# A hybrid encoder block with 64 experts on one core: gathers and scatters of all 128 rows under a bound, gate and up weights split by matrix

## The chip, the cores and the metric

One core of a Trainium2 chip runs the whole layer. The metric is device time in microseconds for one execution, the lower the better. The other cores of the chip are idle.

## The reference

One layer of a streaming encoder, on x of (1, 512, 1024) in f32. First a mixing sub-layer (mLSTM heads, sparse attention, output projection), which the change doesn't touch. Then the channel sub-layer, a mixture of experts, cut to its core here:

```python
scores = jax.nn.sigmoid(hf @ w_router)                    # (512, 64)
# group-limited top 8 of 64 experts per token -> eidx, gw
def body(y, args):
    tok_b, g_b, e_b = args
    xb = hf[tok_b]
    u = jax.nn.silu(xb @ w_gate[e_b]) * (xb @ w_up[e_b])
    yb = (u @ w_down[e_b]) * g_b[:, None]
    return y.at[tok_b].add(yb), None
shared = (jax.nn.silu(hf @ ws_gate) * (hf @ ws_up)) @ ws_down
```

512 tokens times 8 experts are 4096 rows over 64 experts, 64 on average. Routing depends on the data. Run on its own inputs, the reference sends 37 to 100 tokens to an expert: experts 0 to 3 get 59, 51, 73 and 37, experts 26 to 31 get 45, 83, 83, 76, 78 and 43. Each expert has a gate and an up matrix of 1024 x 256 and a down matrix of 256 x 1024, 1 MiB each in f32.

## The kernel before, in words

Three stages come first: input projection (`stage_in`), attention (`stage_attention`), output projection and routing (`stage_route`). They take the first 400 us. In `stage_route`, L1217 and L1220 already load the weights of experts 0, 1 and 3 and some down matrices, and L1417 copies the number of tokens of each expert into `count_tab`.

`stage_experts` takes the rest. It handles one expert after the other, e = 0 to 63, eight per turn of a hardware loop (`turns`, L1678). All engines run their own queue of instructions; semaphores tie them together. For expert e:

- **DVE** builds a 0/1 matrix `pick` (L1881), PE multiplies it with token numbers and gates (`find`), and DVE reads out row numbers and gate weights (L1581 to L1584). The first count(e) of the 128 places hold tokens in order, the others get the number 512 + place, beyond the last token.
- **GpSimd (POOL)** gathers these rows of the normalised input from DRAM into `xg` (`gather_rows`, L1586), four experts ahead. Each row is 4 KB and goes to one partition. The number of rows moved comes from the count: `count_of` (L1756) loads it from `count_tab` into a register, `by_size` (L1745) goes down a tree of branches to one of eleven instructions, for 48, 56, ... 128 rows.
- **PE** transposes the rows (L2024). ACT and DVE split them into a high part rounded to fp32r and the low rest (`xhi`, `xlo`, L1810 and L1905), and do the same with the weights (`whi` at L1802, `wlo` at L1901). The product x times gate and up is the sum of three fp32r products: hi hi, lo hi, hi lo.
- **PE** makes gate and up together (`gate_up`, L2034): 24 matmuls of 512 columns (256 of gate, 256 of up) into one bank. The work is split along the contraction: half 0 is chunks 0 to 3 of both matrices, half 1 is chunks 4 to 7. Weight loads from DRAM (`load_half`, L1570), high parts (`high_half`), low parts (`low_half`) and matmuls all go by these halves. A half of a matrix is 4 KB in a row of DRAM per partition.
- **ACT** makes the silu (L1818), DVE the product `u` (L1910), PE transposes it (L2042) and multiplies it with the down matrix in plain f32 (L2089, `s_dn`). ACT and DVE scale the result by the gate weights into `yb`, two buffers (L1851, L1954).
- **GpSimd** adds `yb` to the sums in DRAM with an accumulating scatter (`add_rows`, L1592), as many rows as the size chosen. Rows of the padding go to 128 spare rows behind the 512. Scatter e starts only when scatter e-1 has landed (`s_sc`, L1770), and `yb` of expert e is written only when scatter e-2 has landed. The last two experts are added from SBUF by PE instead.

Transfers of weights all go through SP's queue: four buffers for gate and up, four for down. SP waits until the low part of a half is made, then loads the same half of the expert four ahead; for the down matrix it waits for `s_dn`. Each transfer is spread over the core's 16 DMA engines. GpSimd's indirect transfers use another queue on the same 16 engines. At the end of the stage a last norm and a store follow.

## Time and profile before

| | us |
|---|---|
| median of 3 runs | 1129.77 |
| lowest and highest | 1128.4, 1130.07 |
| the profiled execution, its time | 1132.51 |
| the profiled execution, its span | 1130.7 |
| PE busy | 1037.0 (92%) |
| DVE busy | 836.9 (74%) |
| ACT busy | 521.8 (46%) |
| POOL busy | 234.5 (21%) |

The span runs from the first to the last instruction of one execution; the rest of its time lies around it. Busy time counts instructions that compute or, for POOL, that write the descriptors of an indirect transfer. PE's matmuls are pipelined and their ends are modelled, so PE's busy share is no measure of its speed; the distance of the starts of matmuls is. A DMA share is the mean over the 16 DMA engines of the time in which they had a packet; it can be a little over 1 where packets overlap. "In the median to landing" is the time from the issue of a transfer to its semaphore.

### The profile page before, as it was taken

How to read it: one execution, taken by the hardware profiler on the slowest of the kernel's cores; microseconds unless marked ns; L12 is line 12 of the kernel's file. 1: busy time of each engine (PE TensorE's matmuls, PEld its weight loads, DVE VectorE, ACT ScalarE, POOL GpSimd, SP SyncE). 2: the span in 40 equal slices, each digit the busy share in tenths (PEclk: the TensorE clock that was granted, in tenths of full speed). 3: DMA queues.
4: the chain of work that ended last, by engine and by line, in shares of the span. 5: the costliest groups of instructions: out<-in, count | busy, mean ns of one | idle time of the engine just before them, and what ended most of it. 6: DMA issues, size and time to landing. Idle time of an engine off the chain costs nothing.

```text
span 1130.7 us, 16022 instructions
## 1 busy us (share of the span) xinstructions
PE 1037.0 (92%) x4777; PEld 733.0 (65%) x4778; DVE 836.9 (74%) x1480; ACT 521.8 (46%) x610; POOL 234.5 (21%) x145
## 2 busy tenths in 40 slices
PE   1899997978998989999998999999999999899995
PEld 1898887657446447766775666667766666566662
DVE  4887899886665457787876787778787776676865
ACT  3425463364111145555554554555555454545542
POOL 0000000100000034353321323423222222342210
PEclk9899998989996999999999999999999999999998
DMA  9775300600948078999999999999999999999944
GB/s 358 244 277 178 101 1 1 229 14 13 388 186 327 27 249 269 356 344 343 338 366 348 323 333 344 345 337 329 324 338 333 346 308 339 304 328 334 340 113 152
DMA packets 82999, 297.60 MB, mean 263 GB/s; under 512 B 10799, under 2 KB 23131, under 8 KB 73437
## 3 DMA queue, kind: packets, MB, share of 16 engines
q1 hardware_dynamic: 69188, 259.12, 63.6%
q0 software_dynamic: 12208, 34.62, 13.4%
q10 hardware_dynamic: 1514, 2.97, 0.7%
q14 instruction: 68, 0.56, 0.1%
q8 instruction: 21, 0.34, 0.1%
HBM read 274.71 MB, written 24.12 MB: 264 GB/s over the span
## 4 chain that ended last, share of the span: by engine, by line
DMA 37%; PE 13%; issue 7%; POOLq 3%; DVE 3%; SPq 2%; ACT 1%; POOL 0%; DVEq 0%; ACTq 0%
DMA y_rows<-yb,row_numbers 28%; PE ps L2034 6%; DMA side<-in_w_exp_up 5%; PE ps L2089 4%; DMA main<-in_w_exp_up 2%; POOLq L1757 2%; DMA xg<-h_rows,row_numbers 1%; SPq L1573 1%; PE ps L2024 1%; PE ps L2134 1%; POOLq L1751 1%; ACT w_gate_up_hi L1802 1%; DVE main L2008 0%; DVE w_gate_up_lo L1901 0%; DVE pick L1881 0%
## 5 line engine op out<-in xcount | busy, mean ns | idle before, releaser
L1901 DVE TENSOR_TENSOR w_gate_up_lo<-side,w_gate_up_hi 128x2048 fp32r<-128x2048 f32 x64 | 146.8, 2294 | 78.9 <-ACT w_gate_up_hi L1802 78.8
L1901 DVE TENSOR_TENSOR w_gate_up_lo<-main,w_gate_up_hi 128x2048 fp32r<-128x2048 f32 x64 | 146.7, 2292 | 71.9 <-ACT w_gate_up_hi L1802 71.8
L1594 POOL DMA_INDIRECT y_rows<-yb,row_numbers x62 | 116.2, 1874 | 375.3 <-issue 311.4
L1802 ACT ACTIVATE w_gate_up_hi<-side 128x2048 fp32r<-128x2048 f32 x64 | 122.1, 1910 | 95.5 <-DMA side<-in_w_exp_up 54.1
L1802 ACT ACTIVATE w_gate_up_hi<-main 128x2048 fp32r<-128x2048 f32 x64 | 122.2, 1910 | 91.5 <-PE ps L2034 45.8
L2034 PE MATMUL ps<-w_gate_up_hi,xT_hi 128*128 128x512 f32 x512 | 144.7, 404 | 11.8 <-DVE xT_lo L1905 8.7
L2034 PE MATMUL ps<-w_gate_up_hi,xT_lo 128*128 128x512 f32 x512 | 137.6, 390 | 0.0
L2034 PE MATMUL ps<-w_gate_up_lo,xT_hi 128*128 128x512 f32 x512 | 137.3, 390 | 0.0
L2034 PEld LDWEIGHTS ps<-w_gate_up_hi,xT_hi 128*128 128x128 f32 x512 | 91.4, 189 | 32.1 <-issue 14.2
L2034 PEld LDWEIGHTS ps<-w_gate_up_hi,xT_lo 128*128 128x128 f32 x512 | 96.2, 188 | 21.1
L2034 PEld LDWEIGHTS ps<-w_gate_up_lo,xT_hi 128*128 128x128 f32 x512 | 96.1, 188 | 21.0
L1588 POOL DMA_INDIRECT xg<-h_rows,row_numbers x48 | 81.4, 1695 | 86.6 <-issue 68.1
L1810 ACT ACTIVATE xT_hi<-ps 128x1024 fp32r<-128x1024 f32 x64 | 65.4, 1023 | 46.4 <-PE ps L2024 46.4
L1905 DVE TENSOR_TENSOR xT_lo<-ps,xT_hi 128x1024 fp32r<-128x1024 f32 x64 | 78.0, 1218 | 11.8 <-ACT xT_hi L1810 11.6
L1851 ACT ACTIVATE yb<-ps,found 128x512 f32<-128x512 f32 x64 | 43.9, 685 | 56.9 <-PE ps L2089 36.6
L2024 PE MATMUL ps<-consts,xg 128*128 128x128 f32 x384 | 55.6, 289 | 12.1 <-DMA xg<-h_rows,row_numbers 12.1
L1881 DVE TENSOR_SCALAR pick<-consts,place_in_expert 128x128 bf16<-128x128 f32 x256 | 63.1, 320 | 0.8 <-PEq L1113 0.8
L2089 PE MATMUL ps<-maskb,uT 128*128 128x512 f32 x128 | 60.7, 619 | 0.0
L2089 PE MATMUL ps<-rows,uT 128*128 128x512 f32 x128 | 57.7, 593 | 1.0 <-DVE uT L1914 1.0
L2089 PE MATMUL ps<-main,uT 128*128 128x512 f32 x128 | 57.6, 592 | 0.0
L2089 PE MATMUL ps<-side,uT 128*128 128x512 f32 x128 | 57.6, 593 | 0.0
L1451 PE MATMUL ps<-side,catT 128*128 128x512 f32 x128 | 55.5, 593 | 1.1 <-PEq L730 1.1
(309 smaller groups left out, 1554.9 us busy)
## 6 DMA issues: line engine op xcount, KB each, us to landing
side<-in_w_exp_gate SPq DMA_DIRECT2D x60, 512.0 KB, 9.6
side<-in_w_exp_up SPq DMA_DIRECT2D x60, 512.0 KB, 23.9
main<-in_w_exp_gate SPq DMA_DIRECT2D x60, 512.0 KB, 9.9
main<-in_w_exp_up SPq DMA_DIRECT2D x60, 512.0 KB, 24.6
side<-in_w_ada SPq DMA_DIRECT2D x20, 1024.0 KB, 7.7
main<-in_w_exp_down SPq DMA_DIRECT2D x16, 1024.0 KB, 23.1
maskb<-in_w_exp_down SPq DMA_DIRECT2D x16, 1024.0 KB, 20.4
side<-in_w_exp_down SPq DMA_DIRECT2D x16, 1024.0 KB, 23.6
```

The costliest lines, as they stand in the source:

```text
L1451: ins = nc.tensor.matmul(ps[:, 2 * i + half, :], catT[:, f, i * P:(i + 1) * P], wout[:, f, 512 * half:512 * (half + 1)], start=f == 0, sto ...
L1588: return pool.indirect_dma_start(out=xg[slot][0:rows, :], out_offset=None, in_=G.h2_rows, in_offset=bass.IndirectOffsetOnAxis(ap=sidx[0:ro ...
L1594: return pool.indirect_dma_start(out=G.y_sums, out_offset=bass.IndirectOffsetOnAxis(ap=sidx[0:rows, n:n + 1], axis=0), in_=yb[0:rows, slot ...
L1802: nc.scalar.activation(whi[:, half], wgu[n % RING][:, :, HALF * half:HALF * (half + 1), :] .rearrange("p m c f -> p c m f"), ACT.Copy).the ...
L1810: nc.scalar.activation(xhi[:, :, :], ps[:, 0:2, :].rearrange("p b (c t) -> p (b c) t", t=P)[:, :, 0:CAP], ACT.Copy).then_inc(s_xhi, 1)
L1851: nc.scalar.activation(yb[:, n % 2, 0:512], ps[0:CAP, 4, :], ACT.Copy, scale=found[:, n, 1:2]).then_inc(s_ya, 1)
L1881: ins = nc.vector.tensor_scalar(pick[:, slot, i, :], k[:, K_IOTA:K_IOTA + CAP], posm[:, bass.ds(NT * e + i, 1)], None, ALU.is_equal)
L1901: nc.vector.tensor_tensor(wlo[:, half], src, whi[:, half].bitcast(F32), ALU.subtract).then_inc(s_wlo, 1)
L1905: nc.vector.tensor_tensor(xlo[:, :, :], ps[:, 0:2, :].rearrange("p b (c t) -> p (b c) t", t=P)[:, :, 0:CAP], xhi[:, :, :].bitcast(F32), AL ...
L2024: ins = nc.tensor.transpose(ps[:, c // 4, (c % 4) * P:(c % 4) * P + CAP], xg[n % RING][:, c:D:KC], ident[0:CAP, 0:CAP])
L2034: ins = nc.tensor.matmul(ps[0:CAP, 2 + slot, :], xp[:, HALF * half + c, :], wp[:, half, c].rearrange("p m f -> p (m f)"), start=half == 0 ...
L2089: ins = nc.tensor.matmul(ps[0:CAP, 4 + half, :], uT[:, n % 2, f, :], wd[n % RING][:, f, 512 * half:512 * (half + 1)], start=f == 0, stop=f ...
```

## The change

Two changes at once.

Rows: every gather and every scatter moves all 128 rows, and a bound on the row number (511) has the hardware drop those beyond it. The first four gathers did that already. The count table, the count look-up and the tree of branches go; GpSimd's loop holds no branch.

Weights: the two parts of the work are no longer halves of the contraction, they are the two matrices. Part 0 is gate, part 1 is up. Each is one transfer of 1 MiB with 8 KB in a row per partition, one high part, one low part, and 24 matmuls of 256 columns into a bank of its own (gate in bank 2 or 3, up in bank 6 or 7).

```diff
-        def load_half(eng, e, slot, half, s_half):
-            at = slice(HALF * half, HALF * (half + 1))
-            for m, w in enumerate((w_gate, w_up)):
-                eng.dma_start(wgu[slot][:, m, at, :], w[e].rearrange("(p c) f -> p c f", c=KC)[:, at, :]).then_inc(s_half, 16)
+        def load_matrix(eng, e, slot, m, s_landed):
+            w = (w_gate, w_up)[m]
+            eng.dma_start(wgu[slot][:, m], w[e].rearrange("(p c) f -> p c f", c=KC)).then_inc(s_landed, 16)
...
-        def add_rows(pool, slot, n, rows=CAP):
+        def add_rows(pool, slot, n):
-            return pool.indirect_dma_start(out=G.y_sums, out_offset=bass.IndirectOffsetOnAxis(ap=sidx[0:rows, n:n + 1], axis=0),
-                                           in_=yb[0:rows, slot, :], in_offset=None, compute_op=ALU.add)
+            return pool.indirect_dma_start(out=G.y_sums, out_offset=bass.IndirectOffsetOnAxis(ap=sidx[:, n:n + 1], axis=0),
+                                           in_=yb[:, slot, :], in_offset=None, compute_op=ALU.add,
+                                           bounds_check=SEQ - 1, oob_is_err=False)
...
                         pool.wait_ge(s_xp, e + 1)
                         pool.sem_inc(s_passed, 1)
-                        count = count_of(e + AHEAD)
-                        by_size(count, SIZES, lambda rows: gather_rows(pool, n % RING, (n + AHEAD) % UNROLL, rows).then_inc(s_g[n % RING], 16))
+                        gather_rows(pool, n % RING, (n + AHEAD) % UNROLL).then_inc(s_g[n % RING], 16)
...
                         pool.wait_ge(s_sc, SC0 + 16 * e)
                         pool.sem_inc(s_passed, 1)
-                        count = count_of(e)
-                        by_size(count, SIZES, lambda rows: add_rows(pool, n % 2, n, rows).then_inc(s_sc, 16))
+                        add_rows(pool, n % 2, n).then_inc(s_sc, 16)
...
-                    nc.scalar.activation(whi[:, half], wgu[n % RING][:, :, HALF * half:HALF * (half + 1), :]
-                                         .rearrange("p m c f -> p c m f"), ACT.Copy).then_inc(s_whi, 1)
+                    nc.scalar.activation(whi[:, m], wgu[n % RING][:, m], ACT.Copy).then_inc(s_whi, 1)
...
-                    act.wait_ge(s_gu, 2 * e + 2)
+                    act.wait_ge(s_gu, 2 * e + 1)
...
                 def multiply(e, slot):
                     dve.wait_ge(s_sg, e + 1)
-                    nc.vector.tensor_tensor(u[:, :], sg[:, :], ps[0:CAP, 2 + slot, DE:2 * DE], ALU.mult).then_inc(s_u, 1)
+                    dve.wait_ge(s_gu, 2 * e + 2)
+                    nc.vector.tensor_tensor(u[:, :], sg[:, :], ps[0:CAP, 6 + slot, DE:2 * DE], ALU.mult).then_inc(s_u, 1)
...
                     pe.wait_ge(s_xlo, e + 1)
-                    for half in range(2):
-                        pe.wait_ge(s_wlo, 2 * e + (half + 1))
+                    for m in range(2):
+                        pe.wait_ge(s_wlo, 2 * e + (m + 1))
+                        if m == 1 and isinstance(e, int) and e == 0:
+                            pe.wait_ge(s_sdc, NT)
                         for j, (xp, wp) in enumerate(((xhi, whi), (xlo, whi), (xhi, wlo))):
-                            for c in range(HALF):
-                                ins = nc.tensor.matmul(ps[0:CAP, 2 + slot, :], xp[:, HALF * half + c, :],
-                                                       wp[:, half, c].rearrange("p m f -> p (m f)"),
-                                                       start=half == 0 and j == 0 and c == 0, stop=half == 1 and j == 2 and c == HALF - 1)
+                            for c in range(KC):
+                                ins = nc.tensor.matmul(ps[0:CAP, 2 + 4 * m + slot, DE * m:DE * (m + 1)], xp[:, c, :], wp[:, m, c, :],
+                                                       start=j == 0 and c == 0, stop=j == 2 and c == KC - 1)
                         ins.then_inc(s_gu, 1)
...
                 gate_up(0, 0)
-                pe.wait_ge(s_sdc, NT)
                 transpose_x(0, 1)
```

The low part, the SP loop, the loads of stage_route and the order of ACT's and DVE's instructions follow the same split: `high_half`, `low_half` and `load_half` became `high_part`, `low_part_of` and `load_matrix` in the same places, with one semaphore for a landed gate matrix and one for an up matrix.

## Rows read from the trace of the kernel before

**Rows 1.** The page, parts 1 and 2: PE's busy time, the 40 slices.

```profile
PE 1037.0 (92%) x4777; PEld 733.0 (65%) x4778; DVE 836.9 (74%) x1480; ACT 521.8 (46%) x610; POOL 234.5 (21%) x145
...
DMA  9775300600948078999999999999999999999944
```

**Rows 2.** POOL's two indirect transfers by line: min/median/max ns; the scatter's landing.

```profile
L1594 POOL DMA_INDIRECT y_rows<-yb,row_numbers x62: 1389/1588/3484, 439.0 to 1098.7; - x62
...
DMA to landing us min/median/max: 4.2/8.6/11.6
...
L1588 POOL DMA_INDIRECT xg<-h_rows,row_numbers x48: 956/1110/3117, 401.5 to 1060.8; - x48
```

**Rows 3.** Windows of the expert stage, first to last scatter, and 500:1000.

```profile
core 0: us, PE busy (x) PEld busy (x) DVE busy (x) ACT busy (x) POOL busy (x), PEclk, DMA share, GB/s
...
439.02:1098.68 659.66, 637.61 (x2805) 441.39 (x2805) 502.14 (x780) 350.06 (x305) 211.67 (x120) 0.99 0.99 328
...
500.00:1000.00 500.00, 482.77 (x2136) 334.89 (x2135) 381.74 (x599) 266.73 (x232) 154.39 (x92) 0.99 1.02 334
```

**Rows 4.** PE: chain and timeline at 434 us; timeline of the projection at 107 us.

```profile
433.67 5.49 PE ps L2034 x24
...
443.68 1.18 PE L2034 MATMUL ps<-w_gate_up_hi,xT_hi 128*128 128x512 f32 x4
...
107.09 1.13 PE L667 MATMUL ps<-w_lo,hT_hi 128*128 128x264 f32 x8
108.06 1.13 PE L667 MATMUL ps<-w_hi,hT_hi 128*128 128x264 f32 x8
```

**Rows 5.** DMA queues, window 500:1000: packets, MB, share of 16 engines.

```profile
q1 hardware_dynamic: 32421, 141.68, 79.4%
q0 software_dynamic: 8725, 25.17, 22.0%
```

**Rows 6.** Chain that ended last, window 560:610: start us, us, what.

```profile
579.27 8.64 DMA y_rows<-yb,row_numbers
...
588.01 0.29 POOLq L1757
...
589.16 0.56 issue
...
589.97 10.18 DMA y_rows<-yb,row_numbers
```

**Rows 7.** Timeline of POOL, 380:440: two of the first four gathers.

```profile
402.96 1.01 POOL L1588 DMA_INDIRECT xg<-h_rows,row_numbers  x1 [0.30 <-issue]
...
416.04 1.00 POOL L1588 DMA_INDIRECT rows<-h_rows,row_numbers  x1 [0.77 <-POOL rows L1739]
```

**Rows 8.** DMA queue q1 in windows 20:28 and then 345:357: packets, MB, share.

```profile
q1 hardware_dynamic: 847, 3.27, 102.6%
...
q1 hardware_dynamic: 695, 5.04, 102.0%
```

**Rows 9.** Windows of 0.2 us in expert 3's gather (columns as in rows 3).

```profile
418.10:418.30 0.20, 0.20 (x3) 0.16 (x2) 0.00 (x0) 0.20 (x1) 0.00 (x0) 1.00 0.53 123
418.30:418.50 0.20, 0.20 (x3) 0.16 (x2) 0.00 (x0) 0.20 (x1) 0.00 (x0) 1.00 0.33 82
418.50:418.70 0.20, 0.20 (x3) 0.16 (x2) 0.00 (x0) 0.20 (x1) 0.00 (x0) 1.00 0.50 205
```

**Rows 10.** Chain that ended last, window 715:775: scatters of experts 27 to 30.

```profile
727.93 10.88 DMA y_rows<-yb,row_numbers
...
740.68 9.57 DMA y_rows<-yb,row_numbers
...
752.04 8.48 DMA y_rows<-yb,row_numbers
...
762.54 8.17 DMA y_rows<-yb,row_numbers
```

**Rows 11.** Groups by line: ACT's high part of weights in the `side` buffers.

```profile
L1802 ACT ACTIVATE w_gate_up_hi<-side 128x2048 fp32r<-128x2048 f32 x64 | 122.1, 1910 | 95.5 <-DMA side<-in_w_exp_up 54.1
```

More of the change, by code:

```diff
@@ L48 @@
 STEPS = (SEQ - 1) // CAP
-MEAN = SEQ * 8 // E_N
-SIZES = [*range(MEAN - 16, CAP, 8), CAP]
 QK_W = 2 * HEADS * DH
@@ L1215, in load_gate_up @@
             def load_gate_up(e):
-                for m, name in enumerate(("w_exp_gate", "w_exp_up")):
-                    sp.dma_start(G.w_gate_up[e][:, m], A[name][0, e].rearrange("(p c) f -> p c f", c=KC)).then_inc(G.s_wgu[e], 16)
+                sp.dma_start(G.w_gate_up[e][:, 0], A["w_exp_gate"][0, e].rearrange("(p c) f -> p c f", c=KC)).then_inc(G.s_wg[e], 16)
+                sp.dma_start(G.w_gate_up[e][:, 1], A["w_exp_up"][0, e].rearrange("(p c) f -> p c f", c=KC)).then_inc(G.s_wu[e], 16)
             def load_down(e):
@@ L1530 @@
 AHEAD = 4
-HALF = KC // 2
 def stage_experts(nc, A, G):
@@ L1584, in pick_rows, with gather_rows @@
             return nc.vector.scalar_tensor_tensor(sidx[:, n:n + 1], f, -1.0, pad[:, 0:1], ALU.add, ALU.add)
-        def gather_rows(pool, slot, n, rows=CAP):
-            return pool.indirect_dma_start(out=xg[slot][0:rows, :], out_offset=None, in_=G.h2_rows,
-                                           in_offset=bass.IndirectOffsetOnAxis(ap=sidx[0:rows, n:n + 1], axis=0),
+        def gather_rows(pool, slot, n):
+            return pool.indirect_dma_start(out=xg[slot], out_offset=None, in_=G.h2_rows,
+                                           in_offset=bass.IndirectOffsetOnAxis(ap=sidx[:, n:n + 1], axis=0),
                                            bounds_check=SEQ - 1, oob_is_err=False)
-        def add_rows(pool, slot, n, rows=CAP):
-            return pool.indirect_dma_start(out=G.y_sums, out_offset=bass.IndirectOffsetOnAxis(ap=sidx[0:rows, n:n + 1], axis=0),
-                                           in_=yb[0:rows, slot, :], in_offset=None, compute_op=ALU.add)
+        def add_rows(pool, slot, n):
+            return pool.indirect_dma_start(out=G.y_sums, out_offset=bass.IndirectOffsetOnAxis(ap=sidx[:, n:n + 1], axis=0),
+                                           in_=yb[:, slot, :], in_offset=None, compute_op=ALU.add,
+                                           bounds_check=SEQ - 1, oob_is_err=False)
         with ExitStack() as inner:
@@ L1602, in isem @@
                 return inner.enter_context(nc.semaphore(name))
-            s_wgu, s_wd = G.s_wgu, G.s_wd
-            s_wgu2 = [isem(f"second_half_landed{n}") for n in range(RING)]
+            s_wg, s_wu, s_wd = G.s_wg, G.s_wu, G.s_wd
             dch = isem("dve_chain")
@@ L1687, in _ @@
             def _(sp):
-                for n in range(RING):
-                    sp.sem_inc(s_wgu2[n], 32)
                 def step(t, n, ahead):
@@ L1743, in _ @@
                 pool.wait_ge(s_yw, 16 * NT)
-                def by_size(count, sizes, move):
-                    if len(sizes) == 1:
-                        move(sizes[0])
-                        return
-                    half = len(sizes) // 2
-                    with pool.If(count > sizes[half - 1]):
-                        by_size(count, sizes[half:], move)
-                    with pool.Else():
-                        by_size(count, sizes[:half], move)
-                def count_of(e):
-                    return pool.value_load(G.count_tab[0:1, bass.ds(e, 1)], min_val=0, max_val=SEQ)
                 def step(t, n, ahead):
@@ L1895, in read_found, with low_part_of @@
                     pick_rows(q, n, 6 + n % 2).then_inc(s_idx, 1)
-                def low_half(t, n, half):
-                    dve.wait_ge(s_whi, 2 * (UNROLL * t + n) + (half + 1))
-                    src = wgu[n % RING][:, :, HALF * half:HALF * (half + 1), :].rearrange("p m c f -> p c m f")
-                    nc.vector.tensor_tensor(wlo[:, half], src, whi[:, half].bitcast(F32), ALU.subtract).then_inc(s_wlo, 1)
+                def low_part_of(t, n, m):
+                    dve.wait_ge(s_whi, 2 * (UNROLL * t + n) + (m + 1))
+                    nc.vector.tensor_tensor(wlo[:, m], wgu[n % RING][:, m], whi[:, m].bitcast(F32), ALU.subtract).then_inc(s_wlo, 1)
                 def x_low(e):
@@ L2156, in build @@
         G.xt = sb("xt", [P, NT, D])
-        G.s_wgu = [ctx.enter_context(nc.semaphore(f"gate_up_landed{n}")) for n in range(RING)]
+        G.s_wg = [ctx.enter_context(nc.semaphore(f"gate_landed{n}")) for n in range(RING)]
+        G.s_wu = [ctx.enter_context(nc.semaphore(f"up_landed{n}")) for n in range(RING)]
         G.s_wd = [ctx.enter_context(nc.semaphore(f"down_landed{n}")) for n in range(RING)]
```

44 lines of the change are left out of this document (21 added, 23 removed).

## The prediction

> **What bounds the kernel now.** First the page's parts 1 and 2 [rows 1]: TensorE is busy 92% of the span and the DMA line stands at 9 through the expert stage. Two resources look full, so I read that stage alone. The 62 scatter-adds start between 439.0 and 1098.7 us [rows 2]; the window between them [rows 3] is 659.66 us for 61 experts, 10.81 us each, with PE busy 637.61 us and the 16 DMA engines at a share of 0.99. Is 10.81 PE's own pace? No: when it waits for nothing, one expert takes PE 443.68 - 433.67 = 10.01 us [rows 4]. Is it the engines'? From 500 to 1000 us the weight queue q1 takes 79.4% and GpSimd's queue q0 22.0% of them [rows 5], together a little over 1 (packets overlap). Per MB that is 0.794 x 16 x 500 / 141.68 = 44.8 engine-us for weights, and 0.22 x 16 x 500 / 25.17 = 69.9 for gathered and added rows. An expert has 3.146 MB of weights and 0.54 MB of rows: (3.146 x 44.8 + 0.54 x 69.9) / 16 = 11.2 engine-us, over the share of 1.02 in that window [rows 3] is 10.9. So the DMA engines set the pace. A third loop runs just under it: scatter e lands, GpSimd looks up the count and branches, scatter e+1 starts. From 579.27 to 589.97 it is 8.64 us of landing and 2.06 us of look-up, branches and issue [rows 6].
>
> **What the change does to this, part by part.**
>
> **Branches and count look-ups go.** Of the 2.06 us between a landing and the next scatter, some 0.3 us is left: the gap ahead of the gather at 402.96, which follows another with no branch between [rows 7]. That is 1.7 us off the scatter loop. It is not the bound, so by itself it gives nothing that the DMA engines don't allow. The count's copy in the routing stage goes too, one small DVE instruction, counted as 0. GpSimd's own time does not grow: indirect gathers of 128 rows took 1.01 and 1.00 us [rows 7], and the median over all, nearly all of a trimmed number, is 1.11 us [rows 2].
>
> **Gate and up as 8 KB packets.** 20:28 us is a stream of 4 KB packets, 345:357 one of 8 KB [rows 8]: 1.026 x 16 x 8 / 3.27 = 40.2 and 1.020 x 16 x 12 / 5.04 = 38.9 engine-us per MB, 3% less. Two thirds of an expert's weights change size: 3.146 / 16 x 44.8 x 2/3 x 0.03 = 0.18 us per expert. SP issues two transfers where it issued four, behind the same two waits; it is no bound.
>
> **Twice the matmuls, half as wide.** An expert's gate and up become 48 matmuls of 256 columns with 48 weight loads, from 24 of 512. The projection at 107 us is such a stream: 8 matmuls of 264 columns, each with a load of its own, start 0.97 us after the 8 before them [rows 4], 121 ns each; 256 columns are 8/2.4 = 3 ns less, 118. 48 x 118 = 5.66 us against 5.49 [rows 4]: +0.17 us on PE, whose pace becomes 10.2 us. Below 10.8 that is covered by the weights' wait; without that cover it is 64 x 0.17 = 11 us. The silu waits for the gate half alone, and the multiply for both. ACT's next instruction still waits for the second product. On DVE the next x low part stands behind the multiply, as it did, and `u` is wanted only after PE's find, transposes and down product. Counted as 0; were that cover gone, the silu's earlier start would even gain its 0.4 us. The new wait for the shared expert's last bank inside gate_up(0, 0) stood one step later before: at most 1 us, once.
>
> **All 128 rows, with a bound.** This is the large term. The reference's own inputs give 37 to 100 tokens per expert, 64 on average, so half the 128 lines are beyond the bound, and always the last ones. What does the chip make of these? Only expert 3's gather (37 tokens) shows it with nothing beside it: issued at 416.04 us [rows 7] with all 128 rows, its packets pass between 417.9 and 418.9. The engines' share there is 0.53, 0.33, 0.50 [rows 9]. 37 rows spread over 16 engines would be two or three each, and the share near 1 for 0.4 us. A share that never passes about a half says that the rows sit on half the engines and that the other half had only dropped ones. A trimmed gather divides its rows among many engines. With 128 rows on every call, the eight engines that hold rows 0 to 63 get nearly all of both transfers, 8 rows of the gather and 8 of the scatter each, where an even spread would be 4 and 4. Every weight matrix still goes in equal shares over all 16 and is complete when the slowest is, so those eight engines set the pace.
>
> The Trainium skill (DMA: Bandwidth & Descriptors, "The descriptor swizzle") has the same picture: engines 0 to 7 take partitions 0 to 63, each four of the first 32 and four of the next 32. By it engine 0 has exactly 8 rows whenever an expert has over 35 tokens, which is every expert here. The trace's 0.53 agrees.
>
> Price of one expert on such an engine. Rows: 16 x 4096 B = 0.0655 MB at 69.9 is 4.6 us. Weights: 0.1966 MB at 44.8, less 0.18, is 8.6 us. Sum 13.2, over 1.02 is 12.9 us: the upper end. Lower end: weights at the undisturbed 38.9 are 7.65 us, rows at 69.9 x 38.9 / 44.8 = 60.7 are 4.0 us; sum 11.6, over 1.02 is 11.4 us. A check from another row: experts 27 and 28 have 83 tokens each, moved as 88 rows, and 29 and 30 have 76 and 78, moved as 80. Their scatters land after 10.88 and 9.57 us against 8.48 and 8.17, and the scatter-to-scatter steps are 12.75 and 11.36 us against 10.50 for expert 29 [rows 10]. 8 rows more, gathered and added, are 16 x 0.0041 MB x 69.9 / 16 = 0.3 us if spread; here they cost 0.9 to 2.3. The division among engines, not the bytes, must differ. I take 12.1 us, a little under the middle of 11.4 and 12.9: the two dearer steps average 12.05, and total traffic falls to some 3.67 MB / 12.1 us = 303 GB/s from 334 [rows 3], which should ease the packets somewhat.
>
> In the Trainium skill's "Why a DMA increments its semaphore by 16 and not by 1" (same page) the number of engines must divide the rows: 88 rows go to 11 engines with 8 each, 80 to 16 with 5. By it 8 rows per engine, those two experts' load, is what every expert will have; the trace's steps agree.
>
> The scatter loop then has some 10.2 us of landing (mean of the two above) and 0.3 us of issue, 10.5 us, under 12.1: late next are the weights, seen as ACT waiting for them.
>
> **Sum.** The engines are saturated for about 57 of the 61 steps (the last weights land some four experts before the end): 57 x (12.1 - 10.81) = +73.5 us. The tail of 5 experts at PE's pace: +0.9. The start, with no backlog yet: 0 to -1. Total +74 us. The profiled execution took 1132.5 us against a median of 1129.8, 0.2% more; on the median, 1204 us.
>
> **The rivals.**
>
> - **Rows spread anyway** (the dip to 0.5 is from something else; each engine gets real and dropped rows alike). Then the engines gain 0.18 us of packets and 0.1 us of padding rows that the scatter no longer moves, and the scatter loop no longer comes near: 10.5 us per expert, above PE's 10.2. 57 x -0.3 = -17: 1113 us, faster. Against it: rows 9 and 10. For it: nothing but the branches gone. Chance 0.09. By the Trainium skill's fit for one GpSimd transfer (same page, "Anatomy of one DMA"), time goes by bytes alone, 2.0 us + 0.26 MB / 436 GB/s = 2.6 us however rows lie. The trace's 8.6 us [rows 2] does not agree.
> - **Spread, and PE takes the gain.** As above, but the 256-column stream runs worse than the 264-column one (its loads surface): PE at 10.8. 1127 to 1132 us. Chance 0.05.
> - **Skewed but cheap.** The eight engines run at their undisturbed rate, 11.4 us: 57 x 0.6 = +34, 1164 us. The rates of rows 8 speak for it (420 GB/s with nothing else queued, so memory isn't full); that these streams had no rows mixed in speaks against it. Chance 0.18.
> - **Dropped scatter rows cost like real ones.** Only gathers of 128 rows are in this trace; if a scatter-add moves all 128, all 16 engines have 8, at 12.9 us or more: +120, 1250 us. Chance 0.06.
> - **Forecast**, skewed at 11.7 to 12.7 us, 1181 to 1238 us: chance 0.62.
>
> **How the numbers follow.** The likeliest case gives 1204 us. The range takes in its bounds and the cheap skew: 1150 to 1250 us, leaving out the two spread cases and the far part of the last. 0.2% (2.3 us) is about what a measurement of this kernel tells from no change. Faster 0.10 (first rival, and the second's edge), same 0.04, slower 0.86.
>
> **What would show it.** Right: scatters start 12 us apart; the landing median goes from 8.6 to 10 us or more; the engines' mean share falls from 0.99 to about 0.9 while PE falls too, from 97% of the stage to some 85%; GB/s near 300; ACT's waits for weights to land, 54.1 us for the `side` buffers now [rows 11], grow several times; the chain moves from scatters to weight transfers. The loop of landing and issue shows a gap of 0.3 us where 2.06 stood. L2034 of an expert takes 5.66 us. Packets of q0 under 512 B rise by some 60 per gather. Wrong: a share still at 0.99 with steps under 10.8 us (rows spread), or a share near 1 with packets of 4 KB for all 128 rows in scatters.

## The result and the profile after

| | before, beside it | after |
|---|---|---|
| median of 4 runs, us | 1129.92 (1128.4 to 1131.24) | 1166.07 (1161.2 to 1167.6) |
| profiled execution, us (its span) | 1132.5 (1130.7) | 1165.66 (1163.8) |
| ratio, 95% interval | | 1.0313 (1.028 to 1.0346) |

The changed kernel is 36 us slower; 74 us were forecast. The sign came out, and so did the cause: real rows on eight of the 16 DMA engines. The size did not, and what the chain shows is not what the prediction named as late next.

The page of the kernel after: busy time, the DMA line and the packets (parts 1 and 2), HBM traffic, the chain.

```profile
PE 1054.8 (91%) x6313; PEld 826.6 (71%) x6314; DVE 846.1 (73%) x1479; ACT 512.4 (44%) x610; POOL 277.4 (24%) x144
...
DMA  9775200603955269999999888989888899999733
...
DMA packets 71768, 296.22 MB, mean 255 GB/s; under 512 B 15233, under 2 KB 27565, under 8 KB 46893
...
HBM read 289.32 MB, written 39.32 MB: 282 GB/s over the span
...
DMA 50%; PE 9%; issue 4%; DVE 2%; POOLq 1%; ACT 0%; POOL 0%; DVEq 0%
```

Where the DMA line of before stood at 9 through the expert stage [rows 1], eights stand in it now. The bytes did not grow: the 128-row transfers drop their surplus rows.

The scatters by line, with their landing (min/median/max), as in [rows 2]:

```profile
L1588 POOL DMA_INDIRECT y_rows<-yb,row_numbers x62: 1550/1581/3222, 439.7 to 1129.8; - x62
...
DMA to landing us min/median/max: 6.0/10.5/12.1
```

The packed trace (the single packets and semaphore steps behind the views) has one thing more than this line. The scatter's semaphore rises in 16 single steps, as many as there are DMA engines. From 500 to 1000 us the eighth comes 6.9 us after the start of the scatter's instruction, the ninth after 8.6 and the last after 10.5 us (medians). Half of the transfer is done early, half late. In e3 below, where the rows are spread, it is 7.6, 7.6 and 9.0 us. That each step stands for one engine is my reading; it fits the load on eight of them.

61 steps in 1129.8 - 439.7 = 690.1 us are 11.31 us each, where 10.81 stood: +30.4 us. The first scatter starts 0.7 us later, and after the last one the kernel takes 34.0 us against 32.0. 30.4 + 0.7 + 2.0 = 33.1 us is the whole difference of the two spans.

The windows of the expert stage (columns as in [rows 3]: PE, PEld, DVE, ACT, POOL busy, granted clock, DMA share, GB/s):

```profile
439.73:1129.80 690.07, 650.22 (x4278) 526.73 (x4277) 510.89 (x775) 341.59 (x306) 256.25 (x121) 1.00 0.88 312
500.00:1000.00 500.00, 469.48 (x3091) 380.14 (x3090) 372.42 (x577) 245.80 (x219) 189.34 (x87) 1.00 0.90 322
```

Before, the share in 500:1000 was 1.02 [rows 3]. Now it is 0.90, and the stage is longer: by the mean of the 16 engines they are not full.

The DMA queues in the window 500:1000, as in [rows 5]:

```profile
q1 hardware_dynamic: 18976, 138.19, 71.6%
q0 software_dynamic: 12538, 22.75, 18.2%
```

The chain, window 560:610 (start us, us, what), as in [rows 6]:

```profile
567.11 10.56 DMA y_rows<-yb,row_numbers
...
577.81 0.51 issue
...
578.54 10.49 DMA y_rows<-yb,row_numbers
...
589.90 10.95 DMA y_rows<-yb,row_numbers
```

A landing takes 10.5 us where 8.64 stood, and the gap from it to the start of the next scatter's instruction is 578.54 - 577.67 = 0.87 us where 2.06 stood. 0.51 of it is one piece of "issue" (time in which GpSimd waited for nothing that the profile shows), and no look-up or tree of branches is left in it. Landing plus gap are 11.4 us, and that is the pace of the kernel after until its last four steps: (1095.2 - 439.7) / 57 = 11.50 us for the first 57, then 34.5 us for four.

The waits (us in total, times, longest) show who stands behind the scatters:

```profile
POOL y_rows L1588 <- DMA y_rows<-yb,row_numbers: 347.2, 52, 8.6
ACT yb L1825 <- DMA y_rows<-yb,row_numbers: 188.3, 54, 4.7
...
ACT w_gate_up_hi L1777 <- PE ps L2010: 29.2, 14, 4.3
```

ACT waits for the `yb` slot that the scatter of two experts earlier frees. No wait for a weight transfer is left, where 54.1 us stood for the `side` buffers alone [rows 11].

### The profile page after: what moved, and what is told of

It is laid out like the page before. It is cut to its first block, busy times and chain, and to the rows that moved or that the text cites. A ratio compares the mean times of both kernels' runs of the same rounds, so it can differ in the third digit from the quotient of the medians.

```text
span 1163.8 us, 17993 instructions
## 1 busy us (share of the span) xinstructions
PE 1054.8 (91%) x6313; PEld 826.6 (71%) x6314; DVE 846.1 (73%) x1479; ACT 512.4 (44%) x610; POOL 277.4 (24%) x144
## 3 DMA queue, kind: packets, MB, share of 16 engines
HBM read 289.32 MB, written 39.32 MB: 282 GB/s over the span
## 4 chain that ended last, share of the span: by engine, by line
DMA 50%; PE 9%; issue 4%; DVE 2%; POOLq 1%; ACT 0%; POOL 0%; DVEq 0%
DMA y_rows<-yb,row_numbers 48%; PE ps L2010 4%; PE ps L2063 3%; DMA xg<-h_rows,row_numbers 2%; PE ps L1998 1%; PE ps L2108 1%; DVE main L1982 0%; DVE main L1972 0%; PE ps L2027 0%; DVE pick L1855 0%; DVE xt L1983 0%; DVE w_gate_up_lo L1874 0%; POOLq L1741 0%; ACT w_gate_up_hi L1777 0%; PE ps L2017 0%
## 5 line engine op out<-in xcount | busy, mean ns | idle before, releaser
L1588 POOL DMA_INDIRECT y_rows<-yb,row_numbers x62 | 101.3, 1633 | 413.0 <-DMA y_rows<-yb,row_numbers 347.2
L2010 PE MATMUL ps<-w_gate_up_hi,xT_hi 128*128 128x256 f32 x1024 | 148.7, 288 | 1.0 <-DVE xT_lo L1878 1.0
L2010 PE MATMUL ps<-w_gate_up_hi,xT_lo 128*128 128x256 f32 x1024 | 144.5, 284 | 0.0
L2010 PE MATMUL ps<-w_gate_up_lo,xT_hi 128*128 128x256 f32 x1024 | 144.2, 284 | 0.0
L1825 ACT ACTIVATE yb<-ps,found 128x512 f32<-128x512 f32 x64 | 44.1, 689 | 203.9 <-DMA y_rows<-yb,row_numbers 188.3
L2010 PEld LDWEIGHTS ps<-w_gate_up_lo,xT_hi 128*128 128x128 f32 x1024 | 132.9, 193 | 0.0
L2010 PEld LDWEIGHTS ps<-w_gate_up_hi,xT_hi 128*128 128x128 f32 x1024 | 131.5, 191 | 1.7 <-issue 1.7
L2010 PEld LDWEIGHTS ps<-w_gate_up_hi,xT_lo 128*128 128x128 f32 x1024 | 132.7, 193 | 0.0
L1582 POOL DMA_INDIRECT xg<-h_rows,row_numbers x48 | 121.2, 2525 | 39.6 <-DVE row_numbers L1578 26.4
L1928 DVE TENSOR_SCALAR yb<-ps,found 128x512 f32<-128x512 f32 x64 | 47.9, 749 | 33.8 <-DMA y_rows<-yb,row_numbers 28.5
L1998 PEld LDWEIGHTS ps<-consts,xg 128*128 128x128 f32 x384 | 46.6, 194 | 33.8 <-DMA xg<-h_rows,row_numbers 33.7
```

The source lines that it names most:

```text
L1582: return pool.indirect_dma_start(out=xg[slot], out_offset=None, in_=G.h2_rows, in_offset=bass.IndirectOffsetOnAxis(ap=sidx[:, n:n + 1], ax ...
L1588: return pool.indirect_dma_start(out=G.y_sums, out_offset=bass.IndirectOffsetOnAxis(ap=sidx[:, n:n + 1], axis=0), in_=yb[:, slot, :], in_o ...
L1825: nc.scalar.activation(yb[:, n % 2, 0:512], ps[0:CAP, 4, :], ACT.Copy, scale=found[:, n, 1:2]).then_inc(s_ya, 1)
L1928: nc.vector.tensor_scalar(yb[:, n % 2, 512:D], ps[0:CAP, 5, :], found[:, n, 1:2], None, ALU.mult).then_inc(s_yd, 1)
L1998: ins = nc.tensor.transpose(ps[:, c // 4, (c % 4) * P:(c % 4) * P + CAP], xg[n % RING][:, c:D:KC], ident[0:CAP, 0:CAP])
L2010: ins = nc.tensor.matmul(ps[0:CAP, 2 + 4 * m + slot, DE * m:DE * (m + 1)], xp[:, c, :], wp[:, m, c, :], start=j == 0 and c == 0, stop=j == ...
```

## The experiments

Three theories stood at first. A: the two queues take turns packet by packet on each engine, so that rows wait longer behind 8 KB packets than behind 4 KB ones; the loss comes from the weights' part. B, the prediction's: engines 0 to 7 carry all real rows; the loss comes from the rows' part. C: the narrow matmuls cost the time. The rivals that came later are told where they arise. Each experiment's median stands beside runs of the kernel before on the same chip; "step" is the time from the first to the last scatter over the 61 steps between them.

### One part alone: e1 and e2

e1 is the kernel before with the rows' part of the change; e2 is the kernel after with the branches and trimmed transfers put back.

```diff
 e1, GpSimd's loop of the kernel before
-                        count = count_of(e)
-                        by_size(count, SIZES, lambda rows: add_rows(pool, n % 2, n, rows).then_inc(s_sc, 16))
+                        add_rows(pool, n % 2, n).then_inc(s_sc, 16)
...
+                                           bounds_check=SEQ - 1, oob_is_err=False)
```

> The rows part alone: all 128 rows with a bound, no branches, weights in halves of 4 KB packets and 512-column matmuls as before. Theory A (the changed kernel is bound by the loop of scatters: landing 10.6 us, with 8 rows in a row on each of eight DMA engines, plus 0.87 us; each row packet takes turns with a weight packet): the turns are shorter by 0.15 us per row, 8 x 0.15 = 1.2 us, landing 9.4, step 10.3 to 10.6, time 1115 to 1135 us. Theory B (only the depth of 8 rows counts, not the size of the weight packets): step 11.4, 1160 to 1170 us. Theory C (the narrow matmuls cost the time): 1105 to 1130 us, with a step at PE's own 10.0 to 10.3 us.

Measured: 1167.57 us against 1130.30, ratio 1.0335 (1.0291 to 1.0379); step 11.42 us, landing 10.5.

> The weights part alone: gate and up by matrix in 8 KB packets with 256-column matmuls, rows trimmed by count through the tree of branches as before. Theory A: 4.8 rows per engine on average wait 0.15 us more for three quarters of their turns, landing 8.6 to 9.2, the branches' 2.06 us are still there: step 11.1 to 11.4, time 1145 to 1165 us. Theory B: 1125 to 1133 us, since the depth is as before. Theory C: the whole loss, 1160 to 1170 us.

Measured: 1136.61 us against 1130.30, ratio 1.0064 (1.0038 to 1.009); landing 8.7 us, step 10.81 in the profiled execution.

The rows' part alone costs 37 us, as much as the whole change, where B had 1160 to 1170. The weights' part with trimmed transfers costs 6 us in the median of 7 runs. B had at most 1133 for it, so 3.6 us of them are unexplained; the profiled execution (1132.46 us) was the fastest of the seven and shows no longer step. A and C fall: each had 1145 us or more for e2, and 8 KB packets did not lengthen the landing (8.7 against 8.6). The waits of e1 show what is missing in the kernel after:

```profile
ACT w_gate_up_hi L1801 <- DMA side<-in_w_exp_up: 78.5, 33, 4.5
ACT w_gate_up_hi L1801 <- DMA main<-in_w_exp_up: 77.5, 31, 4.7
```

In e1, weights in 4 KB packets are late as well. The two bounds, scatters and weights, lie close to each other; e5 below puts a number on it.

### The same rows over 16 engines: e3, e4 and e6

If eight loaded engines are the cause, the place of a token in its expert must be mapped to a partition so that the first n places fall on all 16 engines. The scatter and the gather stay as they are, 128 rows with a bound; only the one-hot `pick` compares places with another table (built on the host with the constants, landed in the stage of the routing).

```diff
+def place_of(p):
+    engine, turn = 8 * (p >> 6) + (p >> 2 & 7), 4 * (p >> 5 & 1) + (p & 3)
+    return 16 * turn + engine
...
-                        ins = nc.vector.tensor_scalar(pick[:, slot, i, :], k[:, K_IOTA:K_IOTA + CAP],
+                        ins = nc.vector.tensor_scalar(pick[:, slot, i, :], k[:, K_CAUSAL:K_CAUSAL + CAP],
```

The map rests on the order that the Trainium skill gives (DMA: Bandwidth & Descriptors, "The descriptor swizzle"). e3 is the kernel after with it, e4 is e1 with it.

> The changed kernel with one thing different: the places of an expert are dealt out over the partitions so that the first n tokens lie evenly on all 16 DMA engines (largest number of rows on one engine 4.5 on average, from 8). A and B: landing falls by 3.5 rows x 0.64 us = 2.2 us to 8.4 us, the loop (9.3 us) stops binding, PE's 10.2 to 10.5 us does: 1105 to 1120 us. C: 1160 to 1170 us, as the changed kernel.

Measured: 1117.79 us against 1130.30, ratio 0.9897 (0.9855 to 0.994).

> The rows part alone, with the places dealt out evenly over the 16 engines as in the run before, and weights in halves of 4 KB. A and B: neither the loop nor the depth binds; PE's pace of 10.0 us or the DMA engines' total do: 1095 to 1115 us, a little under the spread version with 8 KB packets because PE's 0.26 us per expert is saved. If it is over 1125, something else than the rows' spread made the loss.

Measured: 1099.43 us against 1130.30, ratio 0.9741 (0.9698 to 0.9784).

e3's scatters by line with their landing, then its window, then its chain on the page:

```profile
L1597 POOL DMA_INDIRECT y_rows<-yb,row_numbers x62: 1550/1581/3688, 439.4 to 1079.1; - x62
...
DMA to landing us min/median/max: 4.2/9.0/10.6
```

```profile
500.00:1000.00 500.00, 500.00 (x3340) 407.83 (x3339) 394.89 (x622) 270.67 (x238) 126.84 (x95) 1.00 0.99 350
```

```profile
PE 61%; DVE 2%; DMA 1%; issue 0%; ACT 0%; POOLq 0%; DVEq 0%
```

One permutation of places takes 48 us from the changed kernel: 10.49 us per step, PE busy 500.00 of 500 us, 350 GB/s where 322 stood, and the chain is PE's. The trace agrees with the cited order of the engines: the landing falls to 9.0 us and the gap between the eighth and ninth step of the semaphore is gone. With PE the bound, the narrow matmuls come to light: e3 against e4 is 10.49 against 10.22 us per step, 18 us in all.

e6 leaves more rows on twelve engines than on the other four, to see a dose response:

```diff
-    return 16 * turn + engine
+    return np.where(engine < 12, 12 * turn + engine, 96 + 4 * turn + engine - 12)
```

> The changed kernel with the places dealt over 12 of the 16 DMA engines first (the largest number of rows on one engine is 5.7 on average; 8 in the changed kernel, 4.5 when dealt over 16). If landing goes by that number, and the loop binds only where landing plus 0.9 us exceeds PE's 10.35 us: landing 9.3 to 9.6 us, step 10.4 to 10.6, 1118 to 1128 us. If it is all or nothing (skewed or not), near 1118 or near 1166 us.

Measured: 1117.06 us against 1131.58, ratio 0.9882 (0.9849 to 0.9914), step 10.49: no different from e3. The time gives no dose response, because PE's pace covers whatever the uneven load costs. The landing does: in the packed trace its median from 500 to 1000 us is 9.6 us, between 9.0 (e3) and 10.5 (the kernel after), as was forecast, and the semaphore's first four steps are over by 5.7 us, while the other twelve come from 7.2 us on. GpSimd waits 223.4 us for landings, against 99.6 in e3.

### Pace of the engines or latency of one transfer: e5, e9 and e12

B in itself says two things: a scatter whose 8 rows per engine queue behind weights lands late (latency, and the scatters are serial), or the eight engines have too much work per expert (pace). e5 takes the scatters' order away: even and odd experts add into two results, so that two scatters may be under way. The odd experts' result is not added to the output.

```diff
-            return pool.indirect_dma_start(out=G.y_sums, out_offset=bass.IndirectOffsetOnAxis(ap=sidx[:, n:n + 1], axis=0),
+            return pool.indirect_dma_start(out=(G.y_sums, G.y_odd)[slot], out_offset=bass.IndirectOffsetOnAxis(ap=sidx[:, n:n + 1], axis=0),
...
-                        pool.wait_ge(s_sc, SC0 + 16 * e)
+                        pool.wait_ge(s_sc[n % 2], 16 * (UNROLL // 2 * t + n // 2) + 16)
```

> The changed kernel, with the experts of odd number added into a second array, so that scatter e waits for scatter e-2 and no longer for e-1. The second array starts as a copy of the shared expert's result and is left out of the output: the output lacks the odd experts. Theory L (the loop of scatters, landing 10.5 us plus 0.9 us, sets the changed kernel's step of 11.4 us): the loop is gone, the step falls to what the eight loaded DMA engines allow, 10.9 to 11.3 us, or to PE's 10.3: 1105 to 1155 us, by some 5 us more for the four more stores at the start. Theory E (the eight engines' throughput sets it, and the loop's landing is long because they are full): no gain, 1160 to 1175 us.

Measured: 1153.94 us against 1131.58, ratio 1.0199 (1.0165 to 1.0233). e5's scatters of even experts by line, then its windows of 100 us, then its waits, then two scatters on the timeline of GpSimd:

```profile
L1588 POOL DMA_INDIRECT y_rows<-yb,row_numbers x31: 1558/1582/1632, 440.2 to 1105.2; - x31
```

```profile
500.00:600.00 100.00, 100.00 (x680) 82.41 (x680) 78.63 (x125) 53.42 (x47) 25.14 (x19) 1.00 0.96 338
...
700.00:800.00 100.00, 95.00 (x621) 76.04 (x620) 72.56 (x117) 49.36 (x43) 23.54 (x18) 1.00 0.96 329
800.00:900.00 100.00, 94.22 (x605) 74.30 (x603) 72.95 (x116) 50.49 (x45) 21.99 (x17) 1.00 0.93 318
```

```profile
ACT w_gate_up_hi L1778 <- DMA main<-in_w_exp_gate: 90.9, 18, 5.8
ACT w_gate_up_hi L1778 <- DMA side<-in_w_exp_gate: 90.4, 18, 5.6
```

```profile
650.40 1.58 POOL L1588 DMA_INDIRECT y_rows<-yb,row_numbers  x1 [4.93 <-issue]
...
1072.63 1.58 POOL L1588 DMA_INDIRECT y_odd<-yb,row_numbers  x1 [4.08 <-DVE yb L1930]
```

Without the serial scatters the kernel is 12 us faster. Its mean step, (1105.2 - 440.2) / 60 = 11.08 us, is no pace, for it mixes two stretches. The first 20 steps, up to 650.40 us, take 10.51 us each: PE is busy all the time, and until 640 us ACT waits for no weight. But the up matrices of the `main` buffers land ever later, in the median 17.9 us after their issue in 440:540, 35.1 in 540:640 and 39.2 in 700:1000. What was loaded ahead is being used up. The next 37 steps, up to 1072.63 us, take 11.41 us each, and ACT waits for gate matrices, which is the sign that the prediction had named. 11.41 us per expert is the pace of the eight loaded engines. The kernel after runs at 11.4 to 11.5 with its scatters in order: two bounds that are as good as equal, and the serial scatters cost it time only while weights loaded ahead would last. L's range of the time holds at its edge, but its 10.9 to 11.3 us per step were too low; what E says of the engines is true of the second stretch, and its time was not met.

e9 keeps each transfer as it is in the kernel after, 8 real rows on eight engines, but shifts the places of odd experts by 64 partitions, so that the load changes sides every expert:

```diff
+def place_of(p):
+    return (p + 64) % P
...
-                        ins = nc.vector.tensor_scalar(pick[:, slot, i, :], k[:, K_IOTA:K_IOTA + CAP],
+                        ins = nc.vector.tensor_scalar(pick[:, slot, i, :], k[:, (K_IOTA, K_CAUSAL)[slot]:(K_IOTA, K_CAUSAL)[slot] + CAP],
```

> The changed kernel, with the rows of every odd expert placed from partition 64 on, so that odd experts load the other eight DMA engines. Each single gather or scatter still has 8 rows on each of eight engines, but over two experts all 16 carry the same load. Theory D (landing is set by the depth of one transfer, 8 rows in turn with weight packets): landing stays at 10 to 10.5 us and the step at 11.0 to 11.3, 1150 to 1166 us. Theory F (landing is long because eight engines are full all the time, and depth alone costs little): landing near 9 us, the step PE's 10.5, 1115 to 1125 us.

Measured: 1117.68 us against 1130.43, ratio 0.9894 (0.9859 to 0.993). The timeline of GpSimd (start us, us, what, idle before it):

```profile
628.26 1.58 POOL L1596 DMA_INDIRECT y_rows<-yb,row_numbers  x1 [5.46 <-DMA y_rows<-yb,row_numbers]
...
638.70 1.58 POOL L1596 DMA_INDIRECT y_rows<-yb,row_numbers  x1 [5.39 <-DMA y_rows<-yb,row_numbers]
...
649.44 1.58 POOL L1596 DMA_INDIRECT y_rows<-yb,row_numbers  x1 [5.61 <-DMA y_rows<-yb,row_numbers]
```

e9 is as fast as the full spread (1117.79), as F had it. Its scatters wait for landings, but 10.44 and 10.74 us apart, just at PE's 10.49. The landing (packed trace, median of 500 to 1000 us) is 9.6 us, under the 10.5 of the kernel after and over the 9.0 of e3. So the larger part of the long landing comes from loading the same eight engines for every expert. The 8 rows in one transfer may cost the other 0.6 us; PE's pace hides it.

e12 joins the two, e5's two results (odd experts left out again) and e9's places:

> The run with two arrays of sums (1154 us), with the rows of odd experts placed from partition 64 on. The scatter loop is gone in both; here the load of the DMA engines is even over two experts. The output lacks the odd experts, as before. If the 1154 us were the pace of the eight loaded engines (11.08 us per expert): the even load brings PE's 10.49, 1118 to 1126 us, ACT hardly waits for weights. If they came from something else in that version (the four more stores, the late waits): 1148 to 1158 us.

Measured: 1119.74 us against 1128.83, ratio 0.9925 (0.9896 to 0.9953), step (1069.4 - 440.0) / 60 = 10.49 us. Its window, then its waits:

```profile
500.00:1000.00 500.00, 500.00 (x3343) 408.22 (x3343) 394.87 (x619) 269.90 (x238) 124.58 (x95) 1.00 0.98 350
```

```profile
ACT w_gate_up_hi L1786 <- PE ps L2020: 146.8, 62, 2.8
```

The only difference from e5 is the side on which the odd experts' rows lie, and it takes away 34 us and every wait for weights. That is the load of the eight engines, shown by itself. (The 11.08 us in the text on record are e5's mean of two stretches, as told above.)

### What the branches bring: e7

The kernel after, with the count look-ups and branches back, every leaf of the branch moving all 128 rows with the bound.

```diff
-                        add_rows(pool, n % 2, n).then_inc(s_sc, 16)
+                        count = count_of(e)
+                        by_size(count, SIZES, lambda rows: add_rows(pool, n % 2, n).then_inc(s_sc, 16))
```

> The changed kernel with the count look-ups and the tree of branches put back, every leaf moving all 128 rows with the bound. Theory L: the gap between a landing and the next scatter goes from 0.9 back to 2.1 us, step 12.6: 57 x 1.2 = +68 us, 1225 to 1240 us. Theory E: the gap is idle time of a loop that isn't the bound, 1166 to 1185 us.

Measured: 1201.23 us against 1131.58, ratio 1.0633 (1.0591 to 1.0674). Its chain, window 700:730:

```profile
697.62 8.67 DMA y_rows<-yb,row_numbers
...
706.40 0.29 POOLq L1751
...
708.13 9.88 DMA y_rows<-yb,row_numbers
...
719.94 10.69 DMA y_rows<-yb,row_numbers
```

The branches' removal is worth 35 us in the skewed kernel. The gap is 708.13 - 706.29 = 1.84 us, 0.97 more than after's, but the step is only 0.51 more (11.82 against 11.31), for the landings shorten: in the packed trace their median from 500 to 1000 us is 10.1 us, against 10.5. The share of the engines in that window is 0.86, against 0.90; that their longer pauses shorten the landing is likely, but not shown. The time missed both numbers that were on record: landing is no constant that a longer gap adds to.

### What dropped rows cost, and packets: e8, e10 and e11

e8 is e4 with the 8 KB packets of the change and the 512-column matmuls of before: the whole 2 MB of gate and up is issued behind one wait.

```diff
-                        sp.wait_ge(s_wlo, 2 * e + 1)
-                        load_half(sp, UNROLL * t + (n + RING), n % RING, 0, s_wgu[n % RING])
                         sp.wait_ge(s_wlo, 2 * e + 2)
-                        load_half(sp, UNROLL * t + (n + RING), n % RING, 1, s_wgu2[n % RING])
+                        load_gate_up(sp, UNROLL * t + (n + RING), n % RING, s_wgu[n % RING])
```

> The rows spread over 16 engines and computed by halves of the contraction with 512-column matmuls, as in the fastest run so far (1099 us), with one thing different: each matrix is loaded as one transfer of 8 KB packets, after both halves of its buffer are free. It parts the 18.4 us between that run and the spread version with matrices (1118 us). If these are the narrow matmuls (0.29 us per expert on PE): 1097 to 1102 us. If they are the packets: 1112 to 1120 us.

Measured: 1097.46 us against 1131.58, ratio 0.9708 (0.9675 to 0.974). Its chain:

```profile
PE 62%; DVE 1%; issue 0%; ACT 0%; DVEq 0%
```

It is the fastest of the study, faster than both kernels, but no different from e4 (1099.43, intervals overlap): where PE is the bound, the packets' size does not matter. The 18 us between e3 and e4 are the narrow matmuls, as the first of the two forecasts had it.

e10 is e8 without the spread.

> All 128 rows in their order (rows on eight engines, as in the changed kernel), each matrix loaded in 8 KB packets, computed by halves of the contraction with 512-column matmuls. It is the changed kernel without the narrow matmuls, and the run of the rows part alone with larger packets. If narrow matmuls cost nothing while PE is not the bound: 1158 to 1168 us. If they cost their 0.29 us per expert here too: 1145 to 1152 us. If packets made no difference either: 1167 us, as the rows part alone; its late weights would then be no matter of 4 KB packets.

Measured: 1159.15 us against 1130.43, ratio 1.0259 (1.0222 to 1.0296), no wait of ACT for weights. It lies 7 us under the kernel after (1166.07), which differs from it by the narrow matmuls and the split that goes with them, and 8 us under e1 (1167.57), which differs by the packets. Both are small beside the 37 us of the rows, and they cancel in the change. The first of the three forecasts is met: narrow matmuls cost nothing per step while PE is not the bound. The steps are 11.30 us in e10, (1125.6 - 436.4) / 61, and 11.31 in the kernel after. Its 7 us lie outside them: its first scatter starts 3.3 us earlier, and after its last one it takes 31.4 us against 34.0. Against e1 the steps do differ, 11.30 against 11.42.

e11 is e8 with the scatter's bound taken away: the surplus rows are then really added, to rows of `y_sums` that nothing reads.

```diff
-                                           in_=yb[:, slot, :], in_offset=None, compute_op=ALU.add,
-                                           bounds_check=SEQ - 1, oob_is_err=False)
+                                           in_=yb[:, slot, :], in_offset=None, compute_op=ALU.add)
```

> The fastest kernel so far (rows spread, 8 KB, 512 columns, 1097.5 us) with one thing different: the scatter-add has no bound, so that the rows beyond the count are really added to the spare rows. 8 rows on each of all 16 engines instead of 4.5 real ones. If depth and load on the engines are what a scatter costs: landing 10.5 us or more, all 16 engines as full as the eight were, 1160 to 1200 us. If dropped rows already cost like real ones: no change, 1097 us. The page's count of HBM bytes tells whether it takes dropped rows in (289 MB read, 39 MB written in the bounded runs).

Measured: 1121.74 us against 1130.43, ratio 0.993 (0.9906 to 0.9954), 24 us over e8. It missed both numbers on record, 1097 and 1160 to 1200. Its scatters' landing, then the queues of the page, e11 first, then e8:

```profile
DMA to landing us min/median/max: 6.0/10.0/11.3
```

```profile
q0 software_dynamic: 18304, 49.83, 19.3%
...
HBM read 289.39 MB, written 39.32 MB: 293 GB/s over the span
```

```profile
q0 software_dynamic: 18304, 33.60, 12.6%
...
HBM read 289.39 MB, written 39.32 MB: 300 GB/s over the span
```

The same number of packets, 16 MB more in them. The landing grows to 10.0 us, and the scatter loop, not PE, sets a step of (1084.5 - 437.3) / 61 = 10.61 us. Even so the engines pass 370 GB/s from 500 to 1000 us (share 1.03), where 359 stood in e8. A row beyond the bound is almost free: in e8's packed trace it is a packet of 4 or 8 bytes that takes 0.01 us, and a real row's packet of 4 KB takes 0.25 us.

## Why the prediction was right and where it was wrong

**The bound before was read wrongly.** The prediction put the engines' pace of 10.9 us first and the scatter loop just under it. The packed trace of the kernel before has 54 of 61 scatters starting within 2.4 us of the landing ahead of them. Landing and gap are 8.7 and 2.1 us on average, and their sum is the step of 10.81 us itself. The chain of 500 to 1000 us has the scatters first and weights second:

```profile
by line: DMA y_rows<-yb,row_numbers 55.9%; issue 12.3%; DMA side<-in_w_exp_up 10.8%; PE ps L2034 4.5%; POOLq L1757 3.5%; PE ps L2089 3.1%; SPq L1573 2.5%; DMA xg<-h_rows,row_numbers 1.5%; POOLq L1751 1.2%; PE ps L2024 1.0%; ACT w_gate_up_hi
```

Nor was a share near 1 a ceiling: before passed 334 GB/s at a share of 1.02 [rows 3], e4 358 at 1.02. In e4 rows are spread and branches gone, and the stage falls to PE's pace, 10.22 us per expert; that pace had been put at 10.01 from a single expert [rows 4]. No run spreads the rows and keeps the branches, so what each brought in e4 is not shown. The wrong order did not decide the forecast, which rests on the price of the loaded engines.

**Rows on eight engines.** Right, and shown: e3, e9 and e12 each change only where the rows lie and take the loss away; e2 shows that it isn't the weights' part. The working from a share of a half [rows 9] and from the 88-row experts [rows 10] had the right sign.

**The price of a loaded engine is the step that failed.** The prediction took 12.1 us per expert between 11.4 and 12.9; e5 measured 11.41 in its second stretch, the lower end. The terms themselves were near. e5's own queues in 700:1000:

```profile
q1 hardware_dynamic: 11509, 83.78, 76.9%
q0 software_dynamic: 7590, 13.50, 18.1%
```

By these the prices are 0.769 x 16 x 300 / 83.78 = 44.1 and 0.181 x 16 x 300 / 13.50 = 64.4 engine-us per MB, and 0.1966 x 44.1 + 0.0655 x 64.4 = 12.9 us; 13.2 was the prediction's sum. But they pass in 11.41 us. The prediction divided by 1.02, the overlap that the average share of before shows; by this sum it is 12.9 / 11.41 = 1.13 on a loaded engine. That the recorded times of two queues' packets overlap more where both always have work is my reading, and both prices are means over 16 engines; a share by engine isn't in the views.

The check that moved the choice up to 12.1 was misread. The steps of the 88-row experts, 12.75 and 11.36 us, are 10.88 + 1.87 and 9.57 + 1.79 us [rows 10]: a landing, and the look-up and branches behind it. Their mean of 12.05 was the pace of the scatter loop with the very gap that the change takes away. With 0.87 us in place of that gap it is 10.2 + 0.9 = 11.1 us.

**The scatter loop.** Forecast: 10.2 of landing and 0.3 of issue, 10.5, under the engines' pace. Measured: 10.5 and 0.87, 11.4, no faster than the engines' 11.41. The gap was the error: the row used for it [rows 7] was the idle time of POOL ahead of a gather that followed another, and not the time from a landing to the transfer it releases, in which 0.51 us of issue stand in any case. Hence "late next are the weights, seen as ACT waiting for them" was wrong for the kernel after, where the scatters hold PE back just as much as weights would; it comes true only in e5, where the scatters' order is gone.

**Sum.** The first 57 steps are 11.50 us where (1058.1 - 439.0) / 57 = 10.86 stood, +36.4 us in place of +73.5. The last four take 34.5 us where 40.6 stood, -6.0, and the start and the end add 0.7 and 2.0. The number is that of the rival "skewed but cheap" (1164 us, 11.4 per step, chance 0.18), in part by luck. Its reason, engines at their undisturbed rate, is not what the queues show: weights cost 0.716 x 16 x 500 / 138.19 = 41.5 engine-us per MB in the kernel after, and 38.9 undisturbed.

**Narrow matmuls.** Forecast +0.17 us per expert, covered. On PE an expert's gate and up take 5.75 us where 5.49 stood, +0.26, as the chain of e9 has it:

```profile
602.73 5.75 PE ps L2018 x48
```

The cover held in every step (11.30 us in e10, 11.31 in the kernel after); 7 us show at the start and the end of the stage, and 18 us where PE is the bound (e3 against e4).

**8 KB packets.** Forecast 0.18 us per expert less on the engines. e1 against e10, which also has one wait where e1 has two, says 8 us, 0.12 us per step.

**The signs.** Right: a landing of 10 us or more (10.5) and a share of about 0.9 (0.90). Right in direction, too strong in size: PE busy in 94% of the stage (650.22 of 690.07) from 97%, where 85% was forecast, 322 GB/s and not 300, steps of 11.3 us and not 12. Wrong: the chain stayed with the scatters, 48% of the span, and ACT's waits for weights vanished. Small packets: the page's total can't be set against the 60 per gather of the forecast, for the weights' part takes 10799 - 8879 = 1920 of them away (e2) and dropped scatter rows add 3378 of 8 bytes (e11, which drops none, has none of these). Those of 4 bytes on GpSimd's queue, dropped gather rows among them, rise by 2976 in the packed trace, 50 for each of the 60 changed gathers. GpSimd's own time for a gather, forecast unchanged, rose from 1695 to 2525 ns on average. The missing branches alone don't do it (1594 ns in e1). The packed trace shows what does: after 440 us a gather that starts while DVE makes a low part of weights takes 2.84 us on average, one that starts at another time 1.04 us. In the kernel after 53 of 59 start so, in e1 18. That is off the loop between landings.

**Rivals.** "Rows spread anyway" is out by e3, and "Spread, and PE takes the gain" with it: PE's pace with the narrow matmuls is 10.49 us, not 10.8. "Dropped scatter rows cost like real ones" is out by e11. Left open: how the two queues share one loaded engine, why the landing shortens in e7, and the last 3.6 us of e2.

## What to carry to other kernels

Where an indirect transfer has all 128 partitions but valid rows only in the first ones, permute the places so that the valid rows fall on all 16 engines; here one such table turned a loss of 3.4% (e1) into a gain of 2.6% (e4). Then branches and counts can go, since rows beyond the bound cost next to nothing. A bound isn't read off a mean share: at 0.95 the weights were late (e5), at 1.02 ACT waited for none (e4). Nor is a pace read off a mean step: look first whether a stretch runs on what was loaded ahead.

## What was not expected of the hardware

- From a landing to the start of the next scatter's instruction GpSimd needs 0.87 us (chain of the kernel after), 0.51 us of it issue, with no tree of branches.
- A gather keeps GpSimd busy for 1.04 us, but for up to 3.1 us where it starts while DVE runs `w_gate_up_lo` (2.29 us long): 53 of 59 gathers in the kernel after, 3 of 59 in e9.
- The landing follows the rows on the fullest engine: 9.0 us with 4.5 rows (e3), 9.6 with 5.7 (e6), 10.5 with 8 on the same engines each time (the kernel after), 9.6 with 8 on alternate sides (e9).
- The page's HBM line takes dropped scatter rows in: 39.32 MB written with the bound (e8) and without it (e11), while the DMA packets of e11 hold 16 MB more.
- 256-column matmuls with weight loads of their own start 120 ns apart (5.75 us for 48); two of them cost 11 ns more than one of 512 columns (5.49 us for 24, 229 ns).
